# Part of each gate unit's lower half goes from VectorE to GpSimd, and five convolution taps go to an earlier stretch

## The reference, cut to what matters

```python
def trunk_layer(x, c_vec, lp, ctx_cache, pos):
    shift1, scale1, gate1, shift2, scale2, gate2 = adaln(c_vec, lp['w_ada'], lp['b_ada'])
    h = rms_norm(x, lp['norm1']) * (1 + scale1) + shift1
    conv_in, q_lat, kv_lat, k_rope, gates = split_projection(h @ lp['w_in'])
    conv_out = conv_module(conv_in, ...)      # GLU, depthwise conv of 31 taps, LayerNorm, swish, product
    ...                                       # attention: att
    g_conv, g_att = jnp.split(jax.nn.sigmoid(gates), 2, axis=-1)
    x = x + gate1 * ((g_conv * conv_out + g_att * att) @ lp['w_out'])
    ...                                       # mixture of experts
```

## Time and profile before

| | |
|---|---|
| time, median of 3 | 925.15 us (924.52 to 925.28) |
| the profiled execution | 925.79 us, of which the span is 924.0 us |
| TensorE busy | 898.4 us (97%) |
| VectorE busy | 747.8 us (81%) |
| ScalarE busy | 494.7 us (54%) |
| GpSimd busy | 41.7 us (5%) |

### The profile page before, as it was taken

How to read it: one execution, slowest core, us unless ns; L and a number is a source line. 1 busy time by engine, 2 the same in 40 slices (tenths; PEclk the granted TensorE clock), 3 DMA queues, 4 the chain that set the end, 5 groups by cost and what they waited for, 6 DMA issues and landing times.

```text
span 924.0 us, 14522 instructions
## 1 busy us (share of the span) xinstructions
PE 898.4 (97%) x5510; PEld 758.2 (82%) x5510; DVE 747.8 (81%) x1259; ACT 494.7 (54%) x707; POOL 41.7 (5%) x69
## 2 busy tenths in 40 slices
PE   5999999999999999999999999999999999999998
PEld 4897899868888888888868969996699988888886
DVE  3689899778754999779956998996797489986995
ACT  4344522577322687657754353336754267864872
POOL 0100000060000000000000000003400000000000
PEclk9999999999999999999999999999999999999999
DMA  9953665512464899849939336431152169993971
GB/s 360 419 220 140 228 235 220 182 48 89 185 234 177 321 388 366 318 151 382 362 136 367 122 113 265 188 137 46 47 176 98 46 243 353 377 373 110 366 272 69
DMA packets 29351, 206.36 MB, mean 223 GB/s; under 512 B 3456, under 2 KB 3616, under 8 KB 4832
## 3 DMA queue, kind: packets, MB, share of 16 engines
q1 hardware_dynamic: 28944, 204.46, 58.2%
q0 software_dynamic: 336, 0.95, 0.3%
HBM read 203.66 MB, written 1.74 MB: 222 GB/s over the span
## 4 chain that ended last, share of the span: by engine, by line
PE 79%; DVE 13%; ACT 4%; issue 2%; DMA 1%; POOL 1%; SPq 0%; ACTq 0%; DVEq 0%
PE ps L912 57%; PE ps L899 6%; DVE z L2072 4%; PE ps L923 4%; PE ps L890 3%; DVE w_lo L761 3%; PE ps L1401 2%; PE ps L1218 1%; PE ps L1499 1%; PE ps L1500 1%; PE ps L1206 1%; DVE w_lo L766 1%; ACT w_hi L755 1%; PE ps L1011 1%; DMA cond_sb<-cond 1%
## 5 line engine op out<-in xcount | busy, mean ns | idle before, releaser
L766 DVE TENSOR_TENSOR w_lo<-ring,w_hi 128x2048 fp32r<-128x2048 f32 (+2 forms) x104 | 227.6, 2198 | 16.1 <-ACT w_hi L1806 15.4
L912 PE MATMUL ps<-h_hi,w_hi 128*128 128x384 f32 x576 | 198.6, 345 | 2.1 <-issue 0.7
L912 PE MATMUL ps<-h_hi,w_lo 128*128 128x384 f32 x576 | 193.6, 336 | 0.0
L912 PE MATMUL ps<-h_lo,w_hi 128*128 128x384 f32 x576 | 193.5, 336 | 0.0
L1806 ACT ACTIVATE w_hi<-ring 128x2048 fp32r<-128x2048 f32 x96 | 182.7, 1914 | 12.8 <-PE ps L912 12.5
L2072 DVE SCALAR_TENSOR_TENSOR z<-u,par,z 128x399 f32<-128x399 f32 x240 | 137.2, 629 | 1.4
L912 PEld LDWEIGHTS ps<-h_hi,w_hi 128*128 128x128 f32 x576 | 108.1, 188 | 12.9 <-issue 9.3
L761 DVE TENSOR_TENSOR w_lo<-ring,w_hi 128x2048 fp32r<-128x2048 f32 x40 | 91.5, 2288 | 28.1 <-ACT w_hi L755 28.1
L912 PEld LDWEIGHTS ps<-h_lo,w_hi 128*128 128x128 f32 x576 | 108.2, 188 | 0.5 <-issue 0.5
L912 PEld LDWEIGHTS ps<-h_hi,w_lo 128*128 128x128 f32 x576 | 108.1, 188 | 0.0
L912 PE MATMUL ps<-w_hi,hg_hi 128*128 128x512 f32 x256 | 103.1, 403 | 0.3 <-DVE w_lo L766 0.2
(11 more groups left out here) (282 smaller groups left out, 1358.9 us busy)
## 6 DMA issues: line engine op xcount, KB each, us to landing
ring<-wmoe SPq DMA_DIRECT2D x96, 1024.0 KB, 6.8
ring<-wpre SPq DMA_DIRECT2D x95, 1024.0 KB, 6.8
x<-x SPq DMA_DIRECT2D x2, 768.0 KB, 5.1
x_out<-x SPq DMA_DIRECT2D x4, 384.0 KB, 2.4
ring<-wpre SPq DMA_DIRECT2D x2, 416.0 KB, 10.8
par<-par_in POOLq DMA_DIRECT2D x2, 304.5 KB, 7.4
const<-const_in POOLq DMA_DIRECT2D x1, 162.0 KB, 7.8
const<-const_in SPq DMA_DIRECT2D x1, 156.0 KB, 5.6
```

Of the source, the lines that this page charges most:

```text
L766: return nc.vector.tensor_tensor(out, whole, leading.bitcast(F32), ALU.subtract)
L912: m = mm(out, a, b, start=(start and i == 0 and j == 0), stop=(stop and i == n - 1 and j == 2))
```

## The change

GpSimd makes the last 768 of the 2048 columns of each gate unit's lower half, VectorE the first 1280. A new semaphore, `side_lo`, counts GpSimd's parts; TensorE waits for it ahead of each gate unit, and SP before it refills a gate unit's slot. GpSimd's eight subtractions of a layer stand in its queue behind the two stores and before the probabilities. Of the taps, five go from the last gate stretch to the first.

```diff
+SIDE_COLS = 768
...
-CONV_GATES = [12, 8, 11, 8, 10, 5, 15, 15]
+CONV_GATES = [17, 8, 11, 8, 10, 5, 15, 10]
...
             eng.wait_ge(split_hi, base + (n + 1))
-            nc.vector.tensor_tensor(w_lo[place_of(n)], slot(pre_slot(l, PRE_AT[l][SPLIT[n]])),
-                                    w_hi[place_of(n)].bitcast(F32), ALU.subtract).then_inc(split_lo, 1)
+            used = UNIT - SIDE_COLS if SPLIT[n][0] == "gate" else UNIT
+            nc.vector.tensor_tensor(w_lo[place_of(n)][:, 0:used], slot(pre_slot(l, PRE_AT[l][SPLIT[n]]))[:, 0:used],
+                                    w_hi[place_of(n)][:, 0:used].bitcast(F32), ALU.subtract).then_inc(split_lo, 1)
...
                         sp.wait_ge(split_lo, base + (SPLIT_AT[e] + 2))
+                        if e[0] == "gate":
+                            sp.wait_ge(side_lo, l * KD + (e[1] + 1))
...
                 settle(pool)
+                done = rounds_before(pool, l)
                 nc.gpsimd.memset(u[:, :, :], 0.0).then_inc(u_cleared, 1)
...
                 pool.dma_start(kr_out[l], kr[:, 0, :]).then_inc(ckv_stored, 16)
+
+                base = splits_before(pool, l, done)
+                for c in range(KD):
+                    n = SPLIT_AT[("gate", c)]
+                    pool.wait_ge(split_hi, base + (n + 1))
+                    nc.gpsimd.tensor_tensor(w_lo[place_of(n)][:, UNIT - SIDE_COLS:UNIT],
+                                            slot(pre_slot(l, PRE_AT[l][SPLIT[n]]))[:, UNIT - SIDE_COLS:UNIT],
+                                            w_hi[place_of(n)][:, UNIT - SIDE_COLS:UNIT].bitcast(F32), ALU.subtract
+                                            ).then_inc(side_lo, 1)
...
                     wait_made(pe, base, n)
+                    if kind == "gate":
+                        pe.wait_ge(side_lo, l * KD + (c + 1))
```

More of the change, by code:

```diff
@@ L600, in build @@
         u_cleared = sem("u_cleared")
+        side_lo = sem("side_lo")
         par_loaded = sem("par_loaded")
```

## The result

The changed kernel takes 929.48 us (median of 6 runs, 928.66 to 929.99) against 924.92 us (median of 6) before: the ratio is 1.0045, with a 95% interval from 1.0035 to 1.0055. It is 0.45% slower; 929.5 was forecast, in a range from 923.7 to 932.5. The profiled execution took 929.26 us, its span is 927.4 us.

The account below looks back on a forecast made before the run. TensorE, busy 97% of the span, was taken as the bound, with at most 1.25 us to win; VectorE's holds less saved columns and idle time gave +4.2 us in layer 1 and +0.2 in layer 0: 929.5 us, range 923.7 to 932.5.

Parts of the forecast that it names:

- What bounds the stretch: In the gate units TensorE is nearly always busy; at most about 1.25 us, in layer 1, can be won.
- VectorE is held for GpSimd's piece: At each gate unit VectorE waits out GpSimd's whole 1.7 us, 13.6 us a layer, as their SBUF reads exclude each other.
- GpSimd's piece, 1.7 us: GpSimd's subtraction of 768 columns at each gate unit takes 1.7 us, with 1.47 us as lower bound.
- Columns saved, 0.81 us each: 768 fewer columns take 0.81 us off VectorE's lower half at each gate unit, 6.5 us a layer.
- Layer 1, +4.2 us: VectorE's string grows 7.1 us, idle time swallows 2.9; layer 1's taps end and its mean starts 4.2 us later.
- The stall at unit 5: In layer 1, unit 5's lower half comes at about 599.4 against 597.0 wanted, a stall inside the layer's 4.2 us.
- Layer 0, +0.2 us: Layer 0's string ends 2.4 us later after its idle time, against 2.2 us to spare: mean 0.2 us later.
- The total is the same: Moving five taps, 2.7 us, to the first gate stretch leaves VectorE's total unchanged and only uses idle time early.
- Rival B: In the gate stretches VectorE always takes the ports first and GpSimd starves: about +30 us, 955; chance 0.12.
- The added waits and the DMA queue, nothing: TensorE's extra wait at each gate unit and SP's later slot refills cost nothing.
- rival D: VectorE pays in part for GpSimd's pieces, between 0.8 and 1.4 us a gate unit: 924 to 927.3; chance 0.08.
- A: The likeliest case, as summed: VectorE held 1.7 us at each gate unit, 929.5, own range 927.4 to 932; chance 0.60.

Follow-up runs that it names:

- write_only: Changed kernel, but GpSimd subtracts only 8 of its 768 columns and writes zeros over the other 760, all waits kept: 924.27 us, ratio 0.9987.
- no_relief: Changed kernel, but GpSimd subtracts its columns into a free tile, each piece waiting for the previous, and VectorE makes all 2048: 940.22 us, ratio 1.0157.
- taps_only: Kernel before with only the tap list changed, five taps moved to the first gate stretch, nothing new on GpSimd: 924.32 us, ratio 0.999.
- side_only: Changed kernel with the old list of taps, so only GpSimd's subtractions are new: 932.53 us, ratio 1.0079.
- side1280: Changed kernel with GpSimd taking 1280 columns of each lower half instead of 768: 936.08 us, ratio 1.0119.
- The fill: Changed kernel with nine small products on TensorE ahead of layer 1's wait for the last tap: 928.2 us, ratio 1.0033.

## Why the prediction was right, step by step

- **What bounds the stretch**: right. 1.25 us was all that could be won in it; two kernels won it (1.3 us between the marks, 0.8 to 0.9 in the medians), none more.
- **VectorE is held for GpSimd's piece**: right, and it is the cause. The prediction had seen only the other direction in a row and took this one on argument. Shown from three sides: take away GpSimd's reads and keep its writes and all waits (write_only), and the loss is gone; take away the relief and keep the reads (no_relief), and it is 15 us; change the columns, and the hold follows them. The rule of the Trainium skill on this (SBUF — State Buffer, Who interferes with whom) agrees with it both ways. Whoever has the ports keeps them for the whole length of its instruction, as the rule says; but of the sixteen pieces five had begun and still waited while several later VectorE instructions went ahead of them.
- **GpSimd's piece, 1.7 us**: 1.81 to 2.02 us where it got in at once. VectorE mostly loses less: 1.6 us at a tap (2.0 at the first piece of a layer), 1.3 at a first tap, 1.1 at the query products behind the reciprocal. Sum of layer 1: 12.3 us, where 13.6 stood.
- **Columns saved, 0.81 us each**: right (2.29 to 1.48 us).
- **Layer 1, +4.2 us**: 12.3 - 6.5 - 2.8 = 3.0, and 3.0 were measured (of the idle 2.9 us the 0.17 before the last reduction stayed). The term mis-sized is GpSimd's, by 1.3 us. The stall at unit 5, forecast as 2.4 us (599.4 against 597.0) inside the sum, was 0.80.
- **Layer 0, +0.2 us**: none. By the terms VectorE's string ends 12.3 - 6.5 - 4.7 = 1.1 us later, by the timelines 0.9, with 2.2 to spare.
- **What was missing**: the clock. Behind the mean's longer wait TensorE ran at half speed, 1.6 us that no step had. So the total hit the mark by two errors of opposite sign, 1.2 + 0.2 too much for VectorE and 1.6 too little for TensorE. The forecast of the mechanism stands; the agreement to 0.1 us is luck.
- **"The total is the same" of the moved taps**: true only of the changed kernel's sum, which charges the idle time once. For the list by itself it was wrong, as taps_only shows; the text should have seen there that half of the change gains by itself what the whole was worth at best.
- **Rival B**, starving: real, but in part. Unit 4's piece cost TensorE 0.65 us; in side_only unit 6's of layer 0 cost 0.77. Its chance was for the case in which VectorE always wins, and it doesn't.
- **The added waits and the DMA queue, nothing**: right for the waits as such (write_only has them all). But the sum had GpSimd's part done before VectorE's at every unit, and at unit 4 it was not, which is the 0.65 us above.
- **Sums that don't come out**: rival D's upper end is 8 x 1.4 - 6.5 - 2.9 = 1.8 us above, 927.0 and not 927.3; A, B and the rest make 0.75 for slower, where 0.70 is stated. Neither touches the forecast.

## What to carry to other kernels

Before work goes from VectorE to GpSimd, look at what VectorE runs at that moment: if it is instructions with two inputs in SBUF back to back, GpSimd's reading pieces lie in VectorE's string, not beside it, and a column cost there twice what it saved. GpSimd's writes were free here. And look for idle pieces in the late engine's own string first: moving five taps into one of them took the whole gain, without a second engine. A few microseconds that TensorE waits can cost more than themselves, by the clock behind them.

## What the runs showed of the hardware that was not expected

- Whether GpSimd gets in at once depends on the moment. Eleven of sixteen pieces in the changed kernel did (1.81 to 2.02 us); five waited, up to 5.6 us, through taps that follow each other with about 0.12 us between their streams (an estimate, the pitch of 0.545 us less 399 columns at 1.05 ns), until a reciprocal, an instruction behind a short pause of VectorE, or the first tap behind the key products. Why those five and not the others I can't say: the eleven came late in a VectorE instruction more often, but not always.
- A first tap, one tensor times a scalar plus a scalar with a single SBUF tensor as input, was held as well: 1.77 us instead of 0.48 (at 538.85).
- TensorE's granted clock fell to half (1.2 of 2.4 GHz) about where it took up work after standing still. The low stretch of the changed kernel lasted 3.4 us, from 630.12; TensorE resumed at 630.27:

```profile
628.00:630.00 2.00, 0.00 (x0) 0.00 (x0) 2.00 (x4) 0.88 (x2) 0.00 (x0) 1.00 0.00 0
630.00:632.00 2.00, 1.73 (x3) 1.11 (x4) 0.45 (x2) 0.00 (x0) 0.00 (x0) 0.53 0.00 0
632.00:634.00 2.00, 2.00 (x5) 0.95 (x5) 0.00 (x0) 0.00 (x0) 0.00 (x0) 0.62 0.37 74
634.00:636.00 2.00, 2.00 (x16) 1.64 (x15) 1.16 (x3) 0.72 (x2) 0.00 (x0) 1.00 1.06 446
```

It did so at the mean of layer 1 after waits of 2.42, 3.24 and 5.07 us, not after 1.25, and not in the profiled execution of side1280 after 3.08 us. no_relief shows that neither the place nor the length is a simple rule: in its layer 1 the clock also fell at 598.4, in the middle of the gate products. TensorE had resumed at 596.96 after a wait of 1.94 us, and before that at 585.37 after one of 1.56.

```profile
596.00:598.00 2.00, 1.04 (x6) 1.07 (x7) 1.97 (x2) 0.52 (x1) 1.84 (x2) 1.00 0.00 0
598.00:600.00 2.00, 2.00 (x9) 2.00 (x8) 1.93 (x6) 0.00 (x0) 0.85 (x1) 0.59 0.73 209
```

It does not come in every execution either (a fall of 3.4 us takes 0.002 off the mean clock of a run). Of the changed kernel's six runs one had a mean clock of 1.000 and was the fastest, 928.66 us; the others had 0.997 or 0.998. Of side1280's four, two had 1.000 (935.35 and 935.96 us) and two 0.998 and 0.997 (936.20 and 937.01). The fill shows that TensorE's standing still is a condition; what else decides stays open.
